# One-pass products for the output projection and eleven query blocks, and the routing spread over 36 expert blocks

## The chip, the cores and the metric

The kernel runs on one core of a Trainium2 chip. The metric is the time on the device in microseconds (us). Three runs of the kernel before gave a median of 989.1 us (988.98 to 989.2). A profiled execution stands beside them; all rows below come from it.

## What is computed

One decoder layer over 256 positions of width 1024, in float32. Attention in three groups of heads (block-compressed, selected and windowed; a top-64 selection by an indexer; 256 memory tokens), then an output projection, a normalisation, and PEER: 8 retrieval heads over 128 x 128 experts.

```python
x1 = layer_norm(alpha * x + concat(nsa, dsa, mem) @ w_out)     # 256 x 1024 by 1024 x 1024
qh = (x1 @ w_query).reshape(T, 8, 256)                         # 1024 x 2048: 16 blocks of 128 columns
s1, s2 = qh[..., :128] @ sub_keys_1.T, qh[..., 128:] @ sub_keys_2.T
# top 16 of each, top 16 of their sums: 16 experts and a softmax gate for each head
a = gelu(x1 @ expert_u.T)                                      # here: all 16384 experts, densely
y = (gate_matrix * a) @ expert_v
out = layer_norm(alpha * x1 + y)
```

The kernel doesn't gather experts. It computes all of them and multiplies by a gate matrix that is zero outside the chosen ones.

## The kernel before, in words

**Numbers.** A float32 matmul (`F32`) is run by TensorE as two records. A "one-pass" product takes operands rounded to `F32R`, and one record each. To keep precision an operand is split: ScalarE copies it into an `F32R` tile (its high part), VectorE or GpSimd subtracts that from the original (its low part), and TensorE adds high x high, high x low and low x high. Before the change the input projection, the expert blocks and the expert outputs are computed so; the output projection and the queries are plain `F32`.

**Engines and order.** Each engine has its own instruction list, written out by hand in the order of issue, and waits on semaphores. TensorE's list is the longest: attention units (`scores(u)`, `turn(u)`, `outputs(u)`, 20 of them) with slices of other work between them by `advance(work, n)`: `filler` (rest of the input projection, memory projections), `hidden` (compression), `mix0` and `mix1` (output projection of token blocks 0 and 1, 16 slices each). `turn_out(t, part)` transposes the attention output through PSUM bank 2, ScalarE copies it out (`save_out_turn`), and `mix(t)` multiplies it by `w_out`. VectorE normalises (`norm_sum`, `norm_centre`, `norm_scale`, with a root from ScalarE between), TensorE transposes x1 (`turn_x1`), ScalarE copies it (`save_x1_turn`).

**Queries.** `query(j)`, j = 0 to 31: 16 blocks of 128 columns for token block 0, then the same for token block 1 (the weights are loaded twice, through a ring of seven tiles). A query step is 8 matmuls of 128 columns; the step before's `subkey_scores` follows it. ScalarE saves both. VectorE finds the top 16 of each 128 scores, two query blocks at a time (`subkey_tops`), and `route(t)` combines them.

**Expert blocks.** `expert_in(c)`, c = 0 to 127: 24 one-pass products of 256 columns (8 slices of x1 by three). Its weights are loaded by SyncE into five tiles, high parts by ScalarE (`u_split`, three tiles), low parts by VectorE (`fill`), or by GpSimd for the blocks in `POOL_LOW` (5, 8, ... 23). VectorE still routes while the first blocks run; `FILL_AT` says after which of its steps (`pace`) the low part of which block comes. Before block `NTURN` = 30 TensorE transposes the routes (`turn_routes`, L922); ScalarE saves them (L1212), VectorE makes the tables (L1748, L1750).

**Gate groups.** The gate matrix is built in 64 groups of four tokens. For a group GpSimd writes six or five one-hot tiles of 128 x 128 (L467: two in `pair`; L471: four or three in `hot`), ScalarE scales and writes some (`pairs`), VectorE writes four (L1758), and TensorE does four one-pass products (`gates(g)`). Two buffers hold the one-hots, so GpSimd can be two groups ahead. ScalarE and VectorE take the result out (`save_low`, `gate_group`), and `block_gate(c)` multiplies the newly computed blocks. `GROUP_AT` says before which block each group stands: 64 groups from block 33 to block 123.

**Expert outputs.** `expert_out(c)`: 12 one-pass products of 512 columns a block, with splits of the weights by ScalarE (L1256) and VectorE.

L489 is the helper through which all matmuls but the transposes go; L1079 is `u_split`, L1570 `fill`.

Of the kernel before, what the change touches and what calls it, by code (L numbers as in the profile page):

```python
# [7 lines left out]
F32 = mybir.dt.float32  # L8
# [42 lines left out]
GROUP_AT = [N0 + g * (123 - N0) // 63 for g in range(GN)]  # L51
# [80 lines left out]
A_V = A_ALL - 1024  # L132

# [15 lines left out]
FIRST_HI = (22, 23, 26)  # L149


def peer_layer_kernel(nc, x, xT, memT, positions, w_tok, w_memq, w_memk, w_memv, w1k, w1v, w2k, w2v, peT,
                      w_out, ln1, wq, subk, uT, pv, ln2, consts, out):
    with ExitStack() as ctx:
# [68 lines left out]
        qT = gel[:, 0, :].rearrange("p (b t) -> p b t", b=2)  # L223
# [14 lines left out]
        w_o = ar(A_WOUT, KD * D).rearrange("p (k n) -> p k n", k=KD)  # L238
        ring = ar(A_RING, RING * 1024).rearrange("p (b n) -> p b n", b=RING)
# [5 lines left out]
        oT = [rawf[:, 1024 * t:1024 * (t + 1)] for t in range(T)]  # L245
# [53 lines left out]
        l_ring = [sem(f"l_ring{b}") for b in range(RING)]  # L299
# [21 lines left out]
        topped = sem("topped")  # L321
        g_shift, g_exp, route_ready = sem("g_shift"), sem("g_exp"), sem("route_ready")
# [48 lines left out]

        def v_slot(c):
            return (c + 4) % VR
# [8 lines left out]
        def _(sp):  # L382
# [29 lines left out]
            for j in range(RING - 2):  # L412
                load_query(j)
# [3 lines left out]
            for j in range(RING - 2, RING):  # L417
                load_query(j)
            sp.wait_ge(neg_ready, last_of(1, "dsa") + 1)
            sp.dma_start(xs[:, 1, :], x[:, 1, :]).then_inc(l_x, 16)  # L420
            for j in range(RING, 22):
                load_query(j)
# [4 lines left out]
            for j in range(22, 28):  # L427
                load_query(j)
# [3 lines left out]
            for j in range(28, 4 * PH):  # L432
                load_query(j)
# [21 lines left out]
        def _(pool):  # L455
# [7 lines left out]
            def onehots(g):  # L463
# [8 lines left out]
                ins.then_inc(pool_hot, 1)  # L472

# [13 lines left out]
        def _(pe):  # L487
# [188 lines left out]
            def turn(u):  # L676
# [38 lines left out]
            def turn_out(t, part):  # L715
# [4 lines left out]
                pe.wait_ge(pT_saved, nth("o", t, part))  # L720
                for i in range(4):
# [4 lines left out]
            def mix(t):  # L726
                parts = (0, 1)
                pe.wait_ge(l_wo, 16)
# [4 lines left out]
                for part in parts:  # L733
# [21 lines left out]
            def subkey_scores(j):  # L755
                pe.wait_ge(q_saved, j + 1)
                if j >= 1:
                    pe.wait_ge(sk_saved, j)
                mm(ps[:, 3, 0:P], qT[:, j % 2, :], subk_sb[:, j % 2, :], True, True).then_inc(pe_sk, 1)

            def query(j):
                t = j // (2 * PH)
                if j == 0:
                    pe.wait_ge(l_sk, 16)
                    pe.wait_ge(cmp_added, T)
# [1126 lines left out]
```

## Time and profile before

| | |
|---|---|
| median of runs | 989.1 us |
| the profiled execution's own time | 990.93 us |
| its span (first to last instruction) | 989.1 us |
| TensorE busy | 976.0 us, 99% |
| VectorE, ScalarE, GpSimd busy | 758.3, 531.6, 311.5 us |
| share of the chain that ended last in L489 on TensorE | 87% |
| granted clock of TensorE | 0.997 |

Busy time of TensorE is modelled from pipelined matmuls, and the duration listed for one matmul contains its pipeline; the distance between the starts of successive rows is its pace. In a timeline row "x16" is a run of 16 records, and brackets give idle time before the row and what ended it.

### The profile page before, as it was taken

Reading aid. Unit: us, or ns where it says so; the run is one execution under the profiler, and the core shown is the slowest. Engines: PE = TensorE matmul, PEld = TensorE weight load, DVE = VectorE, ACT = ScalarE, POOL = GpSimd, SP = SyncE. Lnnn points to the kernel's source line nnn. Section 1 sums busy time; section 2 is a strip of 40 time slices with the busy share of each in tenths; the row PEclk is TensorE's granted clock in tenths of the full one; section 3 lists DMA queues with packets and bytes.
Section 4 is the critical chain, followed back from the end, with each engine's and each line's share of the span. In section 5 each row is a group of like instructions: output and inputs, shape, how many; then the busy total and the mean of one; then the engine's idle time right before and its main releaser. Section 6 shows DMA issues by size and latency. Waiting matters only on the chain.

```text
span 989.1 us, 17661 instructions
## 1 busy us (share of the span) xinstructions
PE 976.0 (99%) x6306; PEld 871.3 (88%) x6306; DVE 758.3 (77%) x1875; ACT 531.6 (54%) x1125; POOL 311.5 (31%) x370
## 2 busy tenths in 40 slices
PE   9999999999999999999999999999999999999997
PEld 4888866999999999999999999988888888888885
DVE  4577635799998888889999999666666666666667
ACT  3555432234446888878888887633333333333341
POOL 1000000000220999999999999000000000000000
PEclk9999999999999999999999999999999999999999
DMA  9383201882555445444445444775555656555551
GB/s 327 143 349 129 88 20 56 256 328 99 180 191 173 158 163 171 167 154 165 161 167 165 161 167 154 252 234 192 193 192 195 196 193 196 195 193 192 192 191 43
DMA packets 48807, 176.52 MB, mean 178 GB/s; under 512 B 5185, under 2 KB 6225, under 8 KB 47569
## 3 DMA queue, kind: packets, MB, share of 16 engines
q1 hardware_dynamic: 48320, 173.82, 51.8%
q0 software_dynamic: 400, 1.58, 0.5%
q8 instruction: 51, 0.84, 0.3%
q14 instruction: 36, 0.29, 0.1%
HBM read 174.33 MB, written 1.05 MB: 177 GB/s over the span
## 4 chain that ended last, share of the span: by engine, by line
PE 89%; DVE 7%; DMA 2%; ACT 1%; issue 1%; SPq 1%
PE ps L489 87%; DMA arena<-in_w_tok 2%; DVE lo L1570 1%; PE ps L682 1%; DVE pair L1758 1%; DVE arena L1703 1%; DVE hi L1570 1%; DVE arena L1708 1%; DVE arena L1711 0%; ACT hi L1079 0%; SPq L387 0%; DVE slab L1768 0%; DVE arena L1772 0%; SPq L384 0%; SPq L385 0%
## 5 line engine op out<-in xcount | busy, mean ns | idle before, releaser
L489 PE MATMUL ps<-x1hl,hi 128*128 128x256 f32 x2248 | 374.1, 283 | 0.6 <-DVE hi L1570 0.6
L489 PEld LDWEIGHTS ps<-x1hl,hi 128*128 128x128 f32 x2248 | 330.2, 192 | 1.0 <-DVE hi L1570 0.8
L489 PE MATMUL ps<-hi,ahl 128*128 128x512 f32 x992 | 265.3, 389 | 0.0
L1256 ACT CAST hi<-slab 128x1024 fp32r<-128x1024 f32 x128 | 134.9, 1054 | 204.9 <-PE ps L489 204.9
L489 PE MATMUL ps<-x1hl,lo 128*128 128x256 f32 x824 | 233.1, 283 | 0.0
L489 PEld LDWEIGHTS ps<-hi,ahl 128*128 128x128 f32 x992 | 186.1, 188 | 38.6
L471 POOL TENSOR_SCALAR hot<-slab 128x128 fp32r<-128x128 f32 x224 | 197.5, 896 | 0.0
L489 PEld LDWEIGHTS ps<-x1hl,lo 128*128 128x128 f32 x824 | 158.1, 192 | 0.0
L1791 DVE TENSOR_TENSOR lo<-slab,hi 128x1024 fp32r<-128x1024 f32 x128 | 155.9, 1218 | 0.0
L489 PE MATMUL ps<-lo,ahl 128*128 128x512 f32 x496 | 152.8, 389 | 0.0
L1570 DVE TENSOR_TENSOR lo<-slab,hi 128x1024 fp32r<-128x1024 f32 x97 | 121.9, 1257 | 19.1 <-ACT hi L1079 18.8
L1079 ACT CAST hi<-slab 128x1024 fp32r<-128x1024 f32 x128 | 133.4, 1042 | 0.0
L1803 DVE CAST ahl<-arena 128x256 fp32r<-128x256 f32 x124 | 36.5, 294 | 102.3 <-PE ps L489 102.3
L489 PEld LDWEIGHTS ps<-lo,ahl 128*128 128x128 f32 x496 | 93.1, 188 | 19.3
L467 POOL TENSOR_SCALAR pair<-slab 128x128 fp32r<-128x128 f32 x128 | 95.3, 754 | 30.5 <-DVE slab L1750 26.3
L489 PE MATMUL ps<-arena 128*128 128x128 f32 (+6 forms) x806 | 102.3, 294 | 2.6 <-DVE arena L1301 1.4
L489 PEld LDWEIGHTS ps<-arena 128*128 128x128 f32 (+2 forms) x806 | 91.3, 192 | 10.3 <-issue 6.3
L476 POOL TENSOR_TENSOR lo<-slab,hi 128x1024 fp32r<-128x1024 f32 x6 | 14.4, 2405 | 267.5 <-ACT hi L1079 267.5
L1758 DVE TENSOR_SCALAR pair<-slab 128x128 fp32r<-128x128 f32 x256 | 77.6, 362 | 0.0
L1201 ACT ACTIVATE arena<-ps 128x256 f32<-128x256 f32 (+45 forms) x123 | 36.8, 299 | 46.5 <-PE ps L489 46.5
L1805 DVE TENSOR_TENSOR ahl<-arena,ahl 128x256 fp32r<-128x256 f32 x124 | 52.8, 425 | 4.4
L489 PE MATMUL ps<-arena,slab 128*128 128x512 f32 (+1 forms) x160 | 51.9, 470 | 0.7 <-ACT slab L1051 0.7
(209 smaller groups left out, 989.9 us busy)
## 6 DMA issues: line engine op xcount, KB each, us to landing
slab<-in_uT SPq DMA_DIRECT2D x128, 512.0 KB, 3.3
slab<-in_pv SPq DMA_DIRECT2D x128, 512.0 KB, 3.3
arena<-in_wq SPq DMA_DIRECT2D x32, 512.0 KB, 5.2
arena<-in_w_tok SPq DMA_DIRECT2D x8, 512.0 KB, 9.5
arena<-in_w_out SPq DMA_DIRECT2D x1, 4096.0 KB, 15.6
arena<-in_w_tok SPq DMA_DIRECT2D x1, 2048.0 KB, 15.5
arena<-in_w_tok SPq DMA_DIRECT2D x1, 1792.0 KB, 19.0
slab<-in_xT SPq DMA_DIRECT2D x4, 256.0 KB, 7.5
```

What stands on the lines that cost most here:

```text
L467: ins = nc.gpsimd.tensor_scalar(pair[:, g % 2, q, 1, :], iota, tbl[:, 4 * g + q, 0:1], None, ALU.is_equal)
L471: ins = nc.gpsimd.tensor_scalar(hot2[:, g % 2, q, :], iota, tbl[:, 4 * g + q, 1:2], None, ALU.is_equal)
L476: nc.gpsimd.tensor_tensor(u_rest_of(c), u_raw(c), hi[:, c % UH, :].bitcast(F32), ALU.subtract).then_inc(u_lo_pool, 1)
L489: return nc.tensor.matmul(o, lhsT, rhs, start=start, stop=stop, skip_group_check=True)
L1079: nc.scalar.copy(hi[:, c % UH, :], u_raw(c)).then_inc(u_hi, 1)
L1201: ins = nc.scalar.activation(arena[:, c * S + n:(c + 1) * S], ps[:, c % 2, n:S], ACT.Gelu)
L1256: nc.scalar.copy(hi[:, v_hi_slot(c), :], raw[:, v_slot(c), :]).then_inc(v_hi, 1)
L1570: v.tensor_tensor(u_rest_of(c), u_raw(c), hi[:, c % UH, :].bitcast(F32), ALU.subtract).then_inc(u_lo, 1)
L1758: ins = v.tensor_scalar(pair[:, g % 2, q, part, :], iota, tbl[:, 4 * g + q, 0:1], tbl[:, 4 * g + q, 2 + part:3 + part], ALU.is_equal, ALU. ...
L1791: v.tensor_tensor(lo[:, v_slot(c), :], raw[:, v_slot(c), :], hi[:, v_hi_slot(c), :].bitcast(F32), ALU.subtract).then_inc(v_lo, 1)
L1803: v.tensor_copy(o[:, 0, :], a).then_inc(a_hi, 1)
L1805: v.tensor_tensor(o[:, 1, :], a, o[:, 0, :].bitcast(F32), ALU.subtract).then_inc(a_lo, 1)
```

## The change

**Output projection.** `w_out` is split into high parts (ScalarE, `split_mix`, eight) and low parts (GpSimd, eight); the transposed attention output into high (`save_out_turn`, ScalarE) and low (`low_out`, VectorE, four). Each slice's one product becomes three one-pass products, the low x high ones gathered at every fourth slice. Bank 2 may be used again only after the low part is out.

**Queries.** Of 16 query blocks the first five (`ALONE`) are still computed for each token block alone, in plain `F32`; the other eleven for both token blocks at once, by 24 one-pass products of 256 columns. The order is in `STEPS`: 5 alone for token block 0, 11 joint, 5 alone for token block 1; 21 steps instead of 32 and 21 weight loads. High parts of the weights are ScalarE's (`split_query`), low parts VectorE's for the first five joint steps (`low_query`), GpSimd's for the other six. The x1 split moves ahead: `split_x1` for token block 0, `high_x1` and `low_x1` straight from PSUM for token block 1, and `keep_x1` saves it for the last steps. The second `turn_x1` comes before step 4 instead of step 14. Weights 3 to 5 are loaded after the last attention unit, 6 to 9 after half of `mix1` (`pe_half`), later ones when a tile is free. The searches alternate between the token blocks.

**Routing and groups.** The numbers at the top of the diff. `POOL_LOW` stays as it was. ScalarE's `base_of_sums` moves from blocks 124 and 125 to block 126.

The orders of all lists between the attention units are rearranged; the diff leaves those out but for the end of TensorE's.

```diff
-N0 = 33
-NROUTE = 29
-NTURN = 30
-FILL_AT = (54, 55, 57, 66, 68, 68, 76, 79, 79, 86, 89, 89, 97, 99, 99, 106, 109, 109, 119, 120, 120, 123, 124,
-           124, 127, 128, 129, 130, 131,)
+N0 = 40
+NROUTE = 36
+NTURN = 37
+FILL_AT = (59, 61, 72, 73, 74, 74, 77, 78, 78, 80, 81, 81, 83, 84, 84, 86, 89, 89, 96, 99, 99, 106, 109, 109,
+           119, 120, 122, 123, 124, 125, 126, 127, 128, 129, 130, 131,)
 GN = S // 4
 UR, UH = 5, 3
 VR, VH = 8, 4
-GROUP_AT = [N0 + g * (123 - N0) // 63 for g in range(GN)]
+GROUP_AT = [N0 + g * (125 - N0) // 63 for g in range(GN)]
...
+ALONE = 5
+A_WQH, WQH = A_EQ, 5
+A_MORE, MORE = A_WQH + WQH * D, 3
+OWN = ALONE + 5
+assert A_MORE + MORE * D <= A_WMQ
+STEPS = ([(0, j) for j in range(ALONE)] + [(T, j) for j in range(ALONE, 2 * PH)]
+         + [(1, j) for j in range(ALONE)])
+SCORED = [(t, j) for who, j in STEPS for t in range(T) if who in (t, T)]
...
-FIRST_HI = (22, 23, 26)
+FIRST_HI = (18, 19, 21)
...
-            def load_query(j):
-                if j >= RING:
-                    sp.wait_ge(pe_q, j - RING + 1)
-                sp.dma_start(ring[:, j % RING, :], wq[j % (2 * PH)]).then_inc(l_ring[j % RING], 16)
+            def load_query(n):
+                if n >= RING + MORE:
+                    sp.wait_ge(pe_q, n - RING - MORE + 1)
+                elif n >= 6:
+                    sp.wait_ge(pe_half, 1)
+                elif n >= 3:
+                    sp.wait_ge(pe_pv, NU)
+                sp.dma_start(query_raw(n), wq[STEPS[n][1]]).then_inc(query_here(n)[0], 16)
...
+            for k in range(KD):
+                pool.wait_ge(wo_hi, k + 1)
+                nc.gpsimd.tensor_tensor(w_o_lo[:, k, :], w_o[:, k, :], w_o_hi[k // 4][:, k % 4, :].bitcast(F32),
+                                        ALU.subtract).then_inc(wo_lo, 1)
+
+            for n in range(OWN, 2 * PH):
+                pool.wait_ge(q_hi, n - ALONE + 1)
+                nc.gpsimd.tensor_tensor(query_low(n), query_raw(n),
+                                        wq_hi[:, n % WQH, :].bitcast(F32), ALU.subtract).then_inc(q_lo_pool, 1)
...
+                if parts_turned(nth("u", u)):
+                    pe.wait_ge(o_lo, parts_turned(nth("u", u)))
...
                     pe.wait_ge(pT_saved, nth("o", t, part) + 1)
+                    if t == 0:
+                        pe.wait_ge(wo_lo, 4 * part + 4)
                     for half in range(2):
+                        cs = slice(half * 512, (half + 1) * 512)
                         for k in range(4 * part, 4 * part + 4):
-                            first, final = (part, k % 4) == (parts[0], 0), (part, k % 4) == (parts[1], 3)
-                            last = mm(ps[:, 4 * (1 - t) + half, :], oT[t][:, k * P:(k + 1) * P],
-                                      w_o[:, k, half * 512:(half + 1) * 512], first, final)
-                            if final:
+                            a_high, a_low = (o[:, t, k * P:(k + 1) * P] for o in (oT_hi, oT_lo))
+                            w_high, w_low = w_o_hi[part][:, k % 4, cs], w_o_lo[:, k, cs]
+                            if half == 0 and k % 4 == 3:
+                                pe.wait_ge(o_lo, parts_turned(nth("o", t, part)) + 1)
+                            for m, (a, w) in enumerate(((a_high, w_high), (a_high, w_low))):
+                                mm(ps[:, 4 * (1 - t) + half, :], a, w, part == 0 and k == 0 and m == 0, False)
+                            for kl in {0: (), 1: (), 2: (), 3: range(k - 3, k + 1)}[k % 4]:
+                                last = mm(ps[:, 4 * (1 - t) + half, :], oT_lo[:, t, kl * P:(kl + 1) * P],
+                                          w_o_hi[part][:, kl % 4, cs], False, part == 1 and kl == 7)
+                            if k == 7:
                                 last.then_inc(pe_mix, 1)
+                            if t == 1 and half == 1 and k == 3:
+                                last.then_inc(pe_half, 1)
                             yield
...
+            def query(n):
...
+                if n == ALONE:
+                    pe.wait_ge(x1_split, 2 * T)
+                if n == 2 * PH:
+                    pe.wait_ge(x1_kept, 2)
+                pe.wait_ge(*query_here(n))
+                if who == T and n < OWN:
+                    pe.wait_ge(q_lo, n - ALONE + 1)
+                elif who == T:
+                    pe.wait_ge(q_lo_pool, n - OWN + 1)
...
+                    if who < T:
+                        last = mm(ps[:, 4 + n % 2, 0:P], w[:, ks], x1T[who][:, k, :], k == 0, k == KD - 1)
+                    else:
+                        for m, (a, part) in enumerate(((w_high, 0), (w_high, 1), (w_low, 0))):
+                            last = mm(ps[:, 4 + n % 2, 0:S], a[:, ks], x1hl[:, k, part, :], k == 0 and m == 0,
+                                      k == KD - 1 and m == 2)
...
             outputs(19)
             advance(mix0, 1)
             turn_out(1, 0)
-            advance(mix0, 1)
+            advance(mix0, 2)
             advance(mix1, 8)
             turn_out(1, 1)
             advance(mix1, 4)
             turn_x1(0)
             advance(mix1, 4)
-            for j in range(4 * PH):
-                if j == 2 * PH - 2:
+            for n in range(len(STEPS)):
+                if n == ALONE - 1:
                     turn_x1(1)
-                query(j)
-            subkey_scores(4 * PH - 1)
+                query(n)
+            subkey_scores(len(STEPS) - 1)
...
+            def split_mix(k):
+                act.wait_ge(l_wo, 16)
+                if k >= 4:
+                    act.wait_ge(pe_memp, 6)
+                nc.scalar.copy(w_o_hi[k // 4][:, k % 4, :], w_o[:, k, :]).then_inc(wo_hi, 1)
...
+            def split_query(n):
+                act.wait_ge(*query_here(n))
+                if n == ALONE:
+                    act.wait_ge(pe_pv, NU)
+                if n >= ALONE + WQH:
+                    act.wait_ge(pe_q, n - WQH + 1)
+                nc.scalar.copy(wq_hi[:, n % WQH, :], query_raw(n)).then_inc(q_hi, 1)
...
             save_out_turn(1, 1)
+            split_query(5)
             root(0)
+            split_query(6)
+            split_query(7)
+            split_query(8)
             save_x1_turn(0)
-            for j in range(4 * PH):
-                if j == 2:
+            split_query(9)
+            for n in range(len(STEPS)):
+                if n in FIRST_HI:
+                    u_split(FIRST_HI.index(n))
+                save_query(n)
+                if n == 0:
                     root(1)
-                if j == 2 * PH - 2:
-                    save_x1_turn(1)
-                if j in FIRST_HI:
-                    u_split(FIRST_HI.index(j))
-                save_query(j)
-            save_scores(4 * PH - 1)
+                if n == ALONE - 2:
+                    high_x1()
+                    keep_x1()
+                if ALONE + WQH <= n + WQH < 2 * PH:
+                    split_query(n + WQH)
+            save_scores(len(STEPS) - 1)
+            if len(STEPS) in FIRST_HI:
+                u_split(2)
...
+                if c == 126:
+                    base_of_sums(0)
+                    base_of_sums(1)
                 if c >= NK - VH:
...
+            low_out(1, 0)
             weights(1, "mem")
             scale_pair(1)
             dve.wait_ge(l_x, 16)
             dve.wait_ge(l_ln1, 16)
             norm_sum(0)
             norm_centre(0)
+            low_out(1, 1)
+            low_query(5)
             norm_scale(0)
+            low_query(6)
+            low_query(7)
+            low_query(8)
+            low_query(9)
             dve.wait_ge(l_x, 32)
             norm_sum(1)
             norm_centre(1)
             norm_scale(1)
```

## Rows read from the trace of the kernel before

**Rows 1.** Windows from first tables to last one-hot; columns: busy us and count per engine.

```profile
core 0: us, PE busy (x) PEld busy (x) DVE busy (x) ACT busy (x) POOL busy (x), PEclk, DMA share, GB/s
320.70:616.20 295.50, 294.28 (x2444) 293.33 (x2443) 272.86 (x620) 247.17 (x650) 290.56 (x352) 1.00 0.49 163
```

**Rows 2.** Timeline of TensorE, output projection, queries, first expert block; columns: start, duration.

```profile
147.81 8.04 PE L489 MATMUL ps<-arena,slab 128*128 128x512 f32 x18
...
155.69 0.60 PE L722 MATMUL ps<-slab 128*128 128x128 f32 x4
...
164.81 3.73 PE L489 MATMUL ps<-arena 128*128 128x128 f32 x32
...
168.60 1.95 PE L489 MATMUL ps<-arena 128*128 128x128 f32 x16
...
170.39 0.39 PE L489 MATMUL ps<-slab,gel 128*128 128x128 f32 x2
...
170.61 1.95 PE L489 MATMUL ps<-arena 128*128 128x128 f32 x16
...
230.60 0.48 PE L489 MATMUL ps<-x1hl,hi 128*128 128x256 f32 x2
```

**Rows 3.** Timeline of TensorE, late gate groups, and a window of the expert outputs.

```profile
609.75 0.64 PE L489 MATMUL ps<-pair,hot 128*128 128x256 f32 x4
...
613.11 0.64 PE L489 MATMUL ps<-pair,hot 128*128 128x256 f32 x4
...
619.35 0.64 PE L489 MATMUL ps<-pair,hot 128*128 128x256 f32 x4
...
634.23 0.63 PE L489 MATMUL ps<-hi,ahl 128*128 128x512 f32 x2
...
640.00:900.00 260.00, 260.00 (x1149) 215.29 (x1148) 177.69 (x288) 101.18 (x96) 0.60 (x1) 1.00 0.60 197
```

**Rows 4.** ScalarE's copy by timeline, groups of the page, and a DMA issue line.

```profile
156.32 0.58 ACT L1051 COPY slab<-ps 128x512 f32<-128x512 f32 x1 [7.72 <-PE ps L722]
...
L1079 ACT CAST hi<-slab 128x1024 fp32r<-128x1024 f32 x128 | 133.4, 1042 | 0.0
...
L476 POOL TENSOR_TENSOR lo<-slab,hi 128x1024 fp32r<-128x1024 f32 x6 | 14.4, 2405 | 267.5 <-ACT hi L1079 267.5
...
arena<-in_wq SPq DMA_DIRECT2D x32, 512.0 KB, 5.2
```

**Rows 5.** GpSimd's one-hots beside VectorE's low part; waits of L467; window of L1570.

```profile
593.05 0.60 POOL L467 TENSOR_SCALAR pair<-slab 128x128 fp32r<-128x128 f32 x1
...
594.21 0.97 POOL L471 TENSOR_SCALAR hot<-slab 128x128 fp32r<-128x128 f32 x1
...
595.15 1.33 POOL L471 TENSOR_SCALAR hot<-slab 128x128 fp32r<-128x128 f32 x1
...
602.00 1.17 POOL L467 TENSOR_SCALAR pair<-slab 128x128 fp32r<-128x128 f32 x2
...
611.56 1.18 POOL L467 TENSOR_SCALAR pair<-slab 128x128 fp32r<-128x128 f32 x2
...
612.72 3.47 POOL L471 TENSOR_SCALAR hot<-slab 128x128 fp32r<-128x128 f32 x4
...
594.71 1.31 DVE L1570 TENSOR_TENSOR lo<-slab,hi 128x1024 fp32r<-128x1024 f32 x1
...
  PE ps L489: 4.1, 7
...
321.40:616.20 294.80, 115.47 (x91) 1.00 0.49 163
```

**Rows 6.** Timelines about the turn of the routes: TensorE, VectorE, GpSimd.

```profile
318.10 0.82 PE L922 MATMUL ps<-slab,arena 128*128 128x128 f32 x6
...
327.39 0.64 PE L489 MATMUL ps<-pair,hot 128*128 128x256 f32 x4
...
320.23 0.41 DVE L1748 CAST slab<-slab 128x256 fp32r<-128x256 f32 x1 [2.89 <-ACT slab L1212]
...
321.43 1.26 POOL L467 TENSOR_SCALAR pair<-slab 128x128 fp32r<-128x128 f32 x2 [26.27 <-DVE slab L1750]
```

More of the change, by code:

```diff
@@ L370, in pool_lows, with parts_turned, query_raw, query_low @@
             return sum(b <= c for b in POOL_LOW)
+        def parts_turned(n):
+            return sum(event[0] == "o" for event in TURNS[:n])
+        def query_raw(n):
+            b = (n + 4) % (RING + MORE)
+            return ring[:, b, :] if b < RING else more[:, b - RING, :]
+        def query_low(n):
+            b = (n + 4) % (RING + MORE)
+            return ring_lo[:, b, :] if b < RING else more_lo[:, b - RING, :]
+        def query_here(n):
+            return l_ring[n % (RING + MORE)], (n // (RING + MORE) + 1) * 16
         def v_slot(c):
@@ L753, in turn_x1, with subkey_scores @@
                     last.then_inc(pe_pT, 1)
[L755 to L763, printed above, removed]
+            def subkey_scores(n):
+                who, j = STEPS[n]
+                pe.wait_ge(q_saved, n + 1)
+                if n >= 1:
+                    pe.wait_ge(sk_saved, sum(2 if w == T else 1 for w, _ in STEPS[:n]))
+                for i in range(2 if who == T else 1):
+                    last = mm(ps[:, 3, i * P:(i + 1) * P], qT[:, n % 2, i * P:(i + 1) * P], subk_sb[:, j % 2, :], True, True)
+                last.then_inc(pe_sk, 1)
@@ L789, in _ @@
             turn_tokens()
[L790 removed]
+            advance(filler, 3)
             index_scores()
[L792 removed]
+            advance(filler, 6)
             scores(0)
[L794 removed]
+            advance(filler, 5)
             scores(2)
             turn(0)
[L797 to L809 removed]
+            advance(filler, 3)
+            outputs(0)
+            turn(1)
+            advance(filler, 3)
+            turn(2)
+            scores(4)
+            outputs(1)
+            advance(filler, 2)
+            outputs(2)
+            advance(filler, 2)
+            turn(3)
+            advance(filler, 4)
             outputs(3)
             advance(filler, 1)
+            turn(4)
             turn_later(0)
@@ L814, in _ @@
             turn_later(1)
-            turn(4)
             advance(filler, 3)
@@ L821, in _ @@
             outputs(4)
+            index_later(0)
             scores(8)
+            outputs(5)
             turn(6)
-            index_later(0)
             turn(7)
-            outputs(5)
             outputs(6)
+            scores(10)
             index_later(1)
+            turn(8)
+            advance(hidden, 4)
             outputs(7)
-            turn(8)
-            scores(10)
-            advance(hidden, 4)
             outputs(8)
@@ L835, in _ @@
             advance(filler, 1)
+            advance(hidden, 8)
+            advance(filler, 2)
+            advance(hidden, 4)
+            advance(filler, 4)
             turn(9)
+            advance(hidden, 8)
+            turn(10)
             advance(hidden, 4)
+            outputs(9)
+            advance(filler, 9)
+            turn(11)
             advance(filler, 1)
-            advance(hidden, 8)
-            advance(filler, 9)
-            advance(hidden, 8)
-            outputs(9)
-            advance(hidden, 4)
-            advance(filler, 5)
-            turn(10)
             scores(12)
-            turn(11)
+            advance(filler, 1)
             outputs(10)
-            advance(filler, 5)
             outputs(11)
+            advance(filler, 2)
+            compress_kv()
             scores(14)
+            advance(filler, 2)
             turn(12)
-            compress_kv()
-            advance(filler, 6)
-            cmp_scores(0)
-            advance(filler, 4)
-            outputs(12)
-            advance(filler, 1)
-            turn(13)
+            advance(filler, 3)
+            cmp_scores(0)
+            advance(filler, 1)
+            outputs(12)
+            turn(13)
+            advance(filler, 6)
+            turn(14)
+            cmp_turn(0)
             scores(16)
-            cmp_turn(0)
-            turn(14)
             outputs(13)
             turn(15)
+            outputs(14)
             cmp_out(0)
-            outputs(14)
             outputs(15)
@@ L1655, in _ @@
             scale_pair(0)
+            low_out(0, 0)
+            low_out(0, 1)
             maxima(18)
@@ L1671, in _ @@
             norm_scale(1)
-            split_x1(0)
-            for b in range(0, 10, 2):
+            split_x1()
+            low_x1()
+            for b in range(0, ALONE, 2):
                 subkey_tops(0, b)
```

218 lines of the change are left out of this document (121 added, 97 removed).

## The prediction

> **What bounds the kernel now.** I read the page first: TensorE is busy for 99% of the span, and nearly the whole chain of waits is its matmuls. An average says nothing about a stage, so next came the windows, from the opening of the gate tables to GpSimd's last one-hot [rows 1]: there TensorE is at 294.3 of 295.5 us and GpSimd at 290.6, VectorE at 272.9. Two engines are full at once, and one that is made faster alone will meet the other. The reader is to see this double bound; the change touches only TensorE's side of it.
>
> Then the timelines, for the real pace of instructions (the listed duration of a matmul contains its pipeline). A query step of before takes 2.01 us, 168.60 to 170.61: 16 records of fp32 in 1.79 and the subkey product in 0.22 [rows 2]. The output projection runs 18 records from 147.81 to 155.69, 0.438 us each [rows 2]. One-pass products are in the trace too: an expert block and a gate group go from 609.75 to 613.11, 28 records of 256 columns in 3.36 us, 0.12 each, so 2.88 a block and 0.48 a group; and with 512 columns 1149 records fill 260 us, 0.226 each [rows 3].
>
> **TensorE's own work.** Output projection: 32 products of two records, 64 x 0.438 = 28.0 us, become 96 x 0.226 = 21.7: 6.3 less. Queries: 32 steps x 2.01 = 64.3 us become 10 single steps (20.1) and 11 joint ones of 24 x 0.12 + 2 x 0.22 = 3.33 (36.6): 7.6 less. Together 13.9 us less, and the expert blocks could start that much earlier than 230.60 [rows 2].
>
> **What of that is lost before the experts.** Three places.
> First, filler. The first half of the projection fills the gaps of attention's last units, in which TensorE waits for copies. Its 14.0 us become 10.9, while a part now needs ScalarE's copy (0.59 [rows 4]) and VectorE's subtraction before bank 2 is free. Bounds: nothing lost, or all 3.1 and 2 waits of 0.7 on top. I take 1.5.
> Second, the first norm. Call H the second turn of token block 1's output; in before it stands at 155.69 and the queries begin at 164.81, H + 9.1 [rows 2]. Now ScalarE has, between that copy and its copy of x1: four high parts of 1.04 us [rows 4] and the root, and three of the four wait for weights whose DMAs are issued only at about H, 5.2 us to landing [rows 4]. By my count: copy until H + 1.2, high part of 5 until 2.3, root 3.9, of 6 to 8 until about 8.1 (landings 1.5 apart), x1 copied at 9.2. TensorE has its own work until 9.2, so the second half's gain of 1.5 us is gone and no more.  If the loads land 3 us later, all of it is on the path.
> Third, the second norm now has only four query steps in front of its turn instead of fourteen. VectorE must do four low parts at 1.27 (115.5 us over 91 [rows 5]) first: x1 ready at about H + 17.6, where TensorE is at H + 17.4; the joint steps start at H + 21.0 where they could at 20.5. I take 1.7 for it, since the copies in between come as late; low bound 0, high bound 5.
> Sum: 13.9 - 1.5 - 1.5 - 1.7 = 9.2. Experts start at 221.4, bounds 216.7 (nothing lost) and 226.
> ScalarE's eight high parts of the output weights (8.3 us) and GpSimd's eight low parts (2.4 each by [rows 4], 19.2) lie beside attention, where GpSimd is empty; I cost them at nothing, and at up to 2 us if exponentials queue behind them. GpSimd's six query low parts, 2.4 in a step of 3.33, are hidden. In VectorE's queue the candidate searches come in pairs per two joint steps and follow TensorE; u blocks 2 and 3 are loaded when the searches of block 0 of the tokens are through, some 3 us before use.
>
> **Routing.** Its time is set by no engine's work but by a place in TensorE's order: the turn of the routes. In before it stands ahead of block 30, at 318.10; VectorE had finished and waited 2.89 us for the saved table; GpSimd's first one-hot follows at 321.43 [rows 6]. That is 90.8 after the expert start. The change puts the turn ahead of block 37: 7 x 2.88 = 20.2 later, 111.0 after the start. VectorE gets seven low parts more (8.8 us) and has 20.2 us more for them. So GpSimd begins at 221.4 + 111.0 = 332.4, 11 us later than now. This is the term that the reader should watch: TensorE has become earlier, GpSimd later.
>
> **The gate groups.** TensorE alone: first group at 96.8 after the start [rows 6], now 117.0; then 85 blocks instead of 90 and 63 groups, 85 x 2.88 + 63 x 0.48 = 275.0; then one group and three blocks (9.1): 401.1 after the start. (Before: 634.23 - 230.60 = 403.6 [rows 2, 3].)
> GpSimd: 64 groups took 321.43 to 616.2, of which 4.1 us were waits for TensorE [rows 5, 6]: 290.7, or 4.54 a group. A one-hot in the clear has a pitch of 0.58 (two from 593.05 to 594.21); beside VectorE's low part at 594.71 the two one-hots take 0.97 and 1.33, and 1.1 us are lost [rows 5]. 352 one-hots x 0.58 = 204; the other 86.5 us over 91 low parts [rows 5] is 0.95 each. With some 87 low parts in the stage: 204 + 83 = 287, or 4.48 a group, against 275.0/63 = 4.37 that TensorE would take. GpSimd is the bound: last one-hot at 332.4 + 287 = 619.4, group 63 at 619.7, + 9.1 = 628.8. Bounds of a low part's toll: 0 (TensorE then binds, 622.5) and the full 1.27 (then 314 us, 656).
> A page of the Trainium skill speaks against this change: GPSIMD Engine Reference, Key points, says that GpSimd shares its SBUF interfaces with VectorE and contends with VectorE's instructions in a 2-port mode or with two SBUF inputs. By that rule the toll at 594.71 was to be expected, and VectorE's gating products and one-hots could tax GpSimd too; what they would do here is in rival C.
> VectorE: 272.9 us less seven low parts and the small products of those blocks, 262 in 287: 91%, but fuller towards the end. ScalarE has 15% to spare.
>
> **The end.** After group 63 come three blocks instead of five, in which ScalarE scales x (four copies, 2.4 us), the first v block lands (3.3 us after its issue) and is split. I count 8.2 us against 8.6 available: nothing, up to 2 us; I add 0.5. The expert outputs are unchanged.
> Sum: 628.8 - 634.2 + 0.5 = -4.9. The profiled execution took 990.93 (span 989.1), so 986.0; the runs' median is 1.8 below it: **984.2 us**.
>
> **Rivals.**
> A. TensorE binds all through, because one-hots dodge the low parts. For: GpSimd waited 7 times for TensorE in before [rows 5]. Against: only 4.1 us, and it now starts 11 us later. 221.4 + 401.1 = 622.5: 978; with nothing lost before the experts, 973.
> B. The stages before the experts give nearly nothing: late weights in front of the x1 copy, then the second norm. Start at 226 to 228, end at 634: 989. For: four weight loads at H; against: my count has TensorE busy beside most of it.
> C. Slower: the gate stage goes at its old pace. One mechanism: VectorE's low parts, gating products and one-hots, packed denser, hold up GpSimd's one-hots more often, and a group needs both engines. The point is 4.60 us a group (332.4 + 294.4 + 9.4 = 636.2, 991). At 4.66: 995. For: the two groups from 602.00 to 611.56 took 4.78 each [rows 5]. Against: the average of all 64 was 4.54, and fewer low parts fall in each now.
> D. GpSimd's low parts do not change: the diff leaves their list as it stood, so from that part of the title comes nothing; in the sum it is 0.
>
> **Chances.** Forecast (980 to 987) 0.53, A 0.15, B 0.14, C 0.18. What a measurement of this kernel tells from no change is about 0.2%, 2 us. Faster than 987.1: most of the forecast, all of A, a little of B: 0.68. Within: 0.15. Slower: C nearly whole, 0.17. Range 978 to 992: A's and C's near ends are in.
>
> **What would show it.** Records of a joint step 0.12 apart, of the projection 0.226. First expert matmul at 219 to 224. First one-hot 111 after it, later than 321.43 on the clock. GpSimd over 98% busy without waits for TensorE, and TensorE with 5 to 8 us of gaps at gate groups, released by GpSimd or VectorE. End of the expert blocks 407 after their start; 401 speaks for A, 413 and more for C. I am wrong if the start does not move, or if GpSimd is seen waiting.

## The result, and the profile after

The changed kernel took 992.72 us in the median of 17 runs (990.16 to 999.2), the kernel before 989.27 us beside it (17 runs, 988.98 to 990.8): a ratio of 1.0045, 95% interval 1.0034 to 1.0057. The forecast was 984.2, faster; it is slower by 3.5 us, outside the range. The profiled execution took 993.19 us, its span is 991.4, 2.3 above the span of before.

The page first: GpSimd is now on the chain that ended last, as the prediction had it, and TensorE is busy 967.4 us, 8.6 less than before. It does less and ends later.

```profile
span 991.4 us, 17517 instructions
...
PE 967.4 (98%) x6250; PEld 871.3 (88%) x6250; DVE 778.6 (79%) x1877; ACT 548.8 (55%) x1130; POOL 341.7 (34%) x384
...
PE 66%; POOL 27%; DVE 3%; DMA 2%; SPq 1%; ACT 1%; issue 1%; DVEq 0%
```

TensorE's timeline gives the milestones, in order: two waits within attention, the second turn of token block 1's output (H of the prediction; 155.69 before [rows 2]), the queries (164.81 [rows 2]), a joint step with its products, the first expert block (230.60 [rows 2]), the turn of the routes (318.10 [rows 6]), the last gate group (619.35 [rows 3]) and the expert outputs (634.23 [rows 3]).

```profile
114.90 1.08 PE L532 MATMUL ps<-slab,arena 128*128 128x32 f32 x8 [1.89 <-DVE arena L1561]
...
132.80 1.12 PE L769 MATMUL ps<-slab 128*128 128x128 f32 x4 [4.59 <-DVE slab L1649]
...
161.53 0.60 PE L769 MATMUL ps<-slab 128*128 128x128 f32 x4
...
170.79 3.81 PE L532 MATMUL ps<-arena 128*128 128x128 f32 x32
...
181.71 0.50 PE L532 MATMUL ps<-x1hl,wq_hi 128*128 128x256 f32 x2
...
182.16 0.40 PE L532 MATMUL ps<-x1hl,wq_hi 128*128 128x256 f32 x2
...
182.52 0.40 PE L532 MATMUL ps<-x1hl,wq_hi 128*128 128x256 f32 x2
...
229.20 0.48 PE L532 MATMUL ps<-x1hl,hi 128*128 128x256 f32 x2
...
335.83 0.82 PE L995 MATMUL ps<-slab,arena 128*128 128x128 f32 x6
...
627.40 0.64 PE L532 MATMUL ps<-pair,hot 128*128 128x256 f32 x4
...
636.52 0.63 PE L532 MATMUL ps<-hi,ahl 128*128 128x512 f32 x2
```

The reader is to take differences. From H to the first expert block are 67.7 us, and 68.9 by the sum. H itself stands at 152.5 by the sum: 155.69, less 4.7 for the 24 of the projection's 32 slices that lie ahead of it (three quarters of 6.3), plus the 1.5 of loss. It came at 161.53, 9.0 us late. So the search is before H. There the timelines of GpSimd and of VectorE (start, duration) stand side by side:

```profile
110.34 2.35 POOL L509 TENSOR_TENSOR w_o_lo<-arena,w_o_hi 128x1024 fp32r<-128x1024 f32 x1 [8.69 <-ACT w_o_hi L1130]
123.48 6.98 POOL L509 TENSOR_TENSOR w_o_lo<-arena,w_o_hi 128x1024 fp32r<-128x1024 f32 x3 [10.79 <-ACT w_o_hi L1130]
```

```profile
110.97 1.75 DVE L1609 TENSOR_SCALAR slab<-slab 128x2 f32<-128x2 f32 x1
...
118.62 0.17 DVE L1609 TENSOR_SCALAR slab<-slab 128x2 f32<-128x2 f32 x1
...
123.80 0.43 DVE L1605 CUSTOM_DVE_ANT_0 arena<-ps,xs 128x256 f32<-128x256 f32 x1 [3.87 <-PE ps L532]
...
124.61 1.26 DVE L1609 TENSOR_SCALAR slab<-slab 128x2 f32<-128x2 f32 x1
...
126.58 1.60 DVE L1609 TENSOR_SCALAR slab<-slab 128x2 f32<-128x2 f32 x1
...
128.32 2.16 DVE L1617 TENSOR_TENSOR slab<-slab 128x8 f32<-128x8 f32 x1
130.52 1.63 DVE L1633 SCALAR_TENSOR_TENSOR slab<-ps,slab 128x64 f32<-128x64 f32 x8
132.06 0.68 DVE L1649 TENSOR_TENSOR slab<-ps,slab 128x512 f32<-128x512 f32 x1
```

An operation on two numbers a partition takes 0.17 us at 118.62, and 1.75, 1.26 and 1.60 beside GpSimd's low parts of `w_out`. Each long one ends where a low part ends: GpSimd's low part of 110.34 at 112.69, VectorE's operation at 112.72; of the three from 123.48 (2.33 each) the ends are at 125.8, 128.1 and 130.46, VectorE's at 125.87, 128.18 and 130.48. The extra times of the last three, 1.09 + 1.43 + 2.0 = 4.5 us, are TensorE's wait of 4.59 at 132.80: it waits for L1649, behind them in VectorE's list. The operation at 123.80, which also reads PSUM, wasn't held.

Nor is every operation within SBUF held. VectorE beside another low part, GpSimd's row first:

```profile
99.29 2.36 POOL L509 TENSOR_TENSOR w_o_lo<-arena,w_o_hi 128x1024 fp32r<-128x1024 f32 x1 [6.56 <-ACT w_o_hi L1130]
99.44 0.43 DVE L1530 MAX8 slab<-xs 128x8 f32<-128x256 f32 x1
100.43 0.20 DVE L1614 RECIPROCAL slab<-slab 128x8 f32<-128x8 f32 x1
100.66 1.01 DVE L1617 TENSOR_TENSOR slab<-slab 128x8 f32<-128x8 f32 x1
```

`MAX8` and `RECIPROCAL` take here what they take elsewhere (0.43, 0.19 to 0.20); the `TENSOR_TENSOR` behind them, 0.17 elsewhere, lasts until GpSimd's end at 101.65.

Then the clock. Windows of 5 us (busy us per engine, then PEclk, TensorE's granted clock as a share of full speed): it was at full speed in all of these in the kernel before. A share of 0.74 or 0.71 in a window that TensorE fills costs 1.3 or 1.5 us.

```profile
110.00:115.00 5.00, 3.11 (x17) 2.31 (x15) 4.44 (x12) 2.03 (x7) 2.35 (x1) 1.00 0.00 0
115.00:120.00 5.00, 5.00 (x28) 4.50 (x29) 3.58 (x14) 1.91 (x6) 0.00 (x0) 0.74 0.00 0
120.00:125.00 5.00, 4.82 (x31) 3.82 (x29) 1.17 (x5) 2.92 (x5) 1.52 (x1) 0.92 0.01 2
125.00:130.00 5.00, 3.20 (x24) 2.96 (x24) 4.93 (x8) 3.61 (x11) 5.00 (x3) 1.00 0.15 39
130.00:135.00 5.00, 2.20 (x10) 1.70 (x12) 4.03 (x13) 0.58 (x1) 0.45 (x1) 0.61 0.18 68
135.00:140.00 5.00, 5.00 (x22) 3.55 (x19) 1.19 (x3) 0.59 (x1) 0.00 (x0) 0.71 0.00 0
```

With and behind the two waits a part of TensorE's time ran at the lower level, 1.2 GHz. Low parts, held operations, waits, clock: four steps. That the waits bring the clock down isn't shown by itself: the kernel before has such a stretch too, in which TensorE was busy throughout and which the changed kernel lacks (1.00 from 100 to 105):

```profile
100.00:105.00 5.00, 5.00 (x22) 4.10 (x24) 0.10 (x1) 2.15 (x5) 0.00 (x0) 0.68 0.72 256
```

### The profile page after: what moved, and what is told of

The parts are those of the page before. It is cut to its first block, busy times and chain, and to the rows that moved or that the text cites. A ratio compares the mean times of both kernels' runs of the same rounds, so it can differ in the third digit from the quotient of the medians.

```text
span 991.4 us, 17517 instructions
## 1 busy us (share of the span) xinstructions
PE 967.4 (98%) x6250; PEld 871.3 (88%) x6250; DVE 778.6 (79%) x1877; ACT 548.8 (55%) x1130; POOL 341.7 (34%) x384
## 4 chain that ended last, share of the span: by engine, by line
PE 66%; POOL 27%; DVE 3%; DMA 2%; SPq 1%; ACT 1%; issue 1%; DVEq 0%
PE ps L532 64%; POOL hot L504 18%; POOL pair L500 9%; DMA arena<-in_w_tok 2%; PE ps L727 1%; SPq L419 0%; DVE slab L1609 0%; DVE arena L1605 0%; SPq L416 0%; DVE xs L1523 0%; PE ps L769 0%; DVE slab L1617 0%; SPq L417 0%; PE ps L807 0%; PE ps L609 0%
## 5 line engine op out<-in xcount | busy, mean ns | idle before, releaser
L504 POOL TENSOR_SCALAR hot<-slab 128x128 fp32r<-128x128 f32 x224 | 193.6, 878 | 0.0
L1707 DVE TENSOR_TENSOR lo<-slab,hi 128x1024 fp32r<-128x1024 f32 x97 | 122.7, 1266 | 17.7 <-ACT hi L1181 17.6
L1321 ACT ACTIVATE arena<-ps 128x256 f32<-128x256 f32 (+43 forms) x125 | 38.1, 305 | 55.5 <-PE ps L532 55.4
L532 PE MATMUL ps<-arena 128*128 128x128 f32 (+7 forms) x454 | 59.4, 311 | 1.7 <-DVE arena L1422 1.4
L509 POOL TENSOR_TENSOR w_o_lo<-arena,w_o_hi 128x1024 fp32r<-128x1024 f32 x8 | 18.9, 2376 | 121.2 <-ACT w_o_hi L1130 121.2
L532 PEld LDWEIGHTS ps<-arena 128*128 128x128 f32 (+2 forms) x454 | 50.2, 194 | 9.2 <-issue 5.5
L532 PE MATMUL ps<-pair,hot 128*128 128x256 f32 x256 | 42.5, 289 | 3.6 <-POOL hot L504 1.6
```

The source lines that it names most:

```text
L504: ins = nc.gpsimd.tensor_scalar(hot2[:, g % 2, q, :], iota, tbl[:, 4 * g + q, 1:2], None, ALU.is_equal)
L509: nc.gpsimd.tensor_tensor(w_o_lo[:, k, :], w_o[:, k, :], w_o_hi[k // 4][:, k % 4, :].bitcast(F32), ALU.subtract).then_inc(wo_lo, 1)
L532: return nc.tensor.matmul(o, lhsT, rhs, start=start, stop=stop, skip_group_check=True)
L1321: ins = nc.scalar.activation(arena[:, c * S + n:(c + 1) * S], ps[:, c % 2, n:S], ACT.Gelu)
L1707: v.tensor_tensor(u_rest_of(c), u_raw(c), hi[:, c % UH, :].bitcast(F32), ALU.subtract).then_inc(u_lo, 1)
```

## Experiments

Ten kernels ran. Theory 1: GpSimd's low parts of `w_out` are what makes H late, by holding VectorE. Rivals: the new order of attention, the other parts of the change, or the low parts merely coming late.

**Queries only.** Everything of the change but the output projection, with the lists of attention in their old order.

```diff
-  a_high x w_high, a_high x w_low, a_low x w_high      # mix(t)
+  oT[t] x w_o, plain F32; no split_mix, no low_out; lists of PE, ACT, DVE as before up to turn_out(1, 0)
```

> Only the query part, the routing over 36 blocks and the group numbers of the change; the output projection in plain F32 and the order of all lists up to it are those of before. Theory 1 (GpSimd's low parts of w_out hold up VectorE in the attention stage) and rival 2 (the new order and the thinner one-pass filler cost the time there) both expect the second turn of token block 1's output at 155.7 as in before, experts 67.7 us behind it at 223.4 (229.2 in the changed kernel), and 407 us from there to the end of the expert blocks: some 986 to 987, 6 less than the changed kernel. If the experts start after 227, the loss lies in the query part and both are wrong.

986.33 us (985.68 to 987.72; ratio 0.997, 0.996 to 0.9981). H at 155.93, experts at 223.86, outputs at 631.03, 407.2 after. So the query, routing and group parts are worth 3 us, and in the changed kernel the projection's part turns them into a loss.

**No low parts of w_out.** The changed kernel; GpSimd's eight low parts are left out, and TensorE multiplies by the high part twice, so this part of the product is missing.

```diff
-  nc.gpsimd.tensor_tensor(w_o_lo[:, k, :], w_o[:, k, :], w_o_hi..., ALU.subtract).then_inc(wo_lo, 1)   # eight times
-  pe.wait_ge(wo_lo, 4 * part + 4)
+  pe.wait_ge(wo_hi, 4 * part + 4)
-  w_high, w_low = w_o_hi[part][:, k % 4, cs], w_o_lo[:, k, cs]
+  w_high, w_low = w_o_hi[part][:, k % 4, cs], w_o_hi[part][:, k % 4, cs]
```

> The changed kernel without GpSimd's eight low parts of w_out; TensorE does as many products as before (high x high twice), so the low parts of w_out are left out of the result. Theory 1: VectorE's small instructions fall back from 1.3 to 2.2 us to 0.2, the wait of 4.6 us before the first output turn goes, and with it the stretches at half clock; the second output turn at 153 to 156 instead of 161.5, time 984 to 987. Rival 2 (order and filler): second turn after 159, time 990 to 993. Rival 3 (ScalarE's high parts queue ahead of its exponentials): as rival 2, since they stay.

983.52 us (982.13 to 987.53; 0.9944, 0.9929 to 0.996). The timeline has H at 150.77, and no wait at the first turn of that output (124.40; 132.80 in the changed kernel):

```profile
112.65 1.08 PE L527 MATMUL ps<-slab,arena 128*128 128x32 f32 x8 [0.31 <-DVE arena L1556]
...
124.40 0.66 PE L764 MATMUL ps<-slab 128*128 128x128 f32 x4
...
150.77 0.60 PE L764 MATMUL ps<-slab 128*128 128x128 f32 x4
```

and VectorE's small operations are short again:

```profile
121.61 0.17 DVE L1604 TENSOR_SCALAR slab<-slab 128x2 f32<-128x2 f32 x1
121.69 0.20 DVE L1609 RECIPROCAL slab<-slab 128x8 f32<-128x8 f32 x1
121.92 0.17 DVE L1612 TENSOR_TENSOR slab<-slab 128x8 f32<-128x8 f32 x1
```

H is 10.8 us earlier, more than theory 1 had asked for. TensorE's full work is there, and so are ScalarE's high parts and the new order: none of these makes H late. The 10.8 by the two traces: 0.7 was there before the first low part (a place in TensorE's list at 56.70 against 56.02, another at 111.11 against 110.44), so that 10.1 are the low parts'. Of these 6.2 are waits (1.89 + 4.59 - 0.31); the other 3.9 fit the clock, some 4.1 by the windows (1.3 + 1.5; 0.4 in 120 to 125, at 0.92; 0.9 in 130 to 135, 0.39 of 2.2 us busy). In this kernel every window of 5 us from 90 to 170 is at full clock.

**Pieces.** The low parts are back on GpSimd, all of them, each cut into eight instructions of 128 columns. It keeps the amount of work and changes only the length of one instruction.

```diff
-  nc.gpsimd.tensor_tensor(w_o_lo[:, k, :], ...).then_inc(wo_lo, 1)
+  for c in range(0, D, 128):
+      ins = nc.gpsimd.tensor_tensor(w_o_lo[:, k, c:c + 128], ...)
+  ins.then_inc(wo_lo, 1)
```

> The changed kernel with each of GpSimd's eight low parts of w_out cut into eight instructions of 128 columns (2.4 us becomes eight of about 0.35). Theory 1, in the form that an instruction of GpSimd with two SBUF inputs shuts VectorE's SBUF-to-SBUF instructions out until it ends: VectorE's small instructions now wait 0.3 us at most, the second output turn comes at 152 to 156 instead of 161.5, experts at 220 to 224, time 984 to 987. Rival 4, that the total of GpSimd's traffic slows VectorE: nothing gained, or worse by the fixed cost of 56 more instructions, 992 to 996.

985.54 us (983.52 to 988.01; 0.9961, 0.9949 to 0.9974). GpSimd's timeline, and then VectorE's:

```profile
121.24 10.03 POOL L511 TENSOR_TENSOR w_o_lo<-arena,w_o_hi 128x128 fp32r<-128x128 f32 x24 [6.62 <-ACT w_o_hi L1133]
```

```profile
123.30 0.51 DVE L1612 TENSOR_SCALAR slab<-slab 128x2 f32<-128x2 f32 x1
123.72 0.19 DVE L1617 RECIPROCAL slab<-slab 128x8 f32<-128x8 f32 x1
123.94 0.27 DVE L1620 TENSOR_TENSOR slab<-slab 128x8 f32<-128x8 f32 x1
```

GpSimd is busy longer (0.42 a piece, 3.4 a low part against 2.35), and yet H comes at 153.43, 8.1 earlier. The longest of the 20 small operations of that line is 0.53 us (1.75 in the changed kernel). That settles how VectorE is held: until the running GpSimd instruction ends.

**Low parts on VectorE.** The whole change, with the low parts in idle places of VectorE's list, and attention in its old order.

```diff
-  GpSimd: eight low parts
+  DVE: low_mix(0..3) between rounds of index_round(1), low_mix(4..7) beside cmp_shift(1)
```

> The whole change, but the eight low parts of w_out are VectorE's, in its idle places, and the lists up to the projection are ordered as in before. Theory 1: nothing shuts VectorE out; second output turn at 152 to 155 (155.9 in the run with the queries alone, less the first half's one-pass gain, plus what ten us more on VectorE push back), experts at 220 to 223, and the gate stage as before 407.3: 984 to 986. Rival 2 (one-pass filler is too thin for the copies behind bank 2): not below 986.

985.25 us (984.53 to 986.29; 0.9963, 0.9949 to 0.9977). H at 152.19, outputs at 627.67. The same result by moving the work (1.22 us a low part on VectorE); its one wait for a low part is 0.85 us.

**Old order, low parts on GpSimd.** The same kernel with the eight low parts given back to GpSimd: against the last one it moves nothing else.

```diff
-  DVE: low_mix(0..7)
+  GpSimd: the loop of the changed kernel
```

> The whole change, w_out's low parts on GpSimd as in it, but the lists of attention in the order of before (those of the kernel with VectorE's low parts, with the low parts taken from VectorE's list). Theory 1 (GpSimd's low parts hold VectorE's small operations, wherever the lists put these): small VectorE operations of over 1 us beside GpSimd's low parts, second turn of token block 1's output at 155 to 161, 987 to 992 us. Rival (it is the new order of attention that makes the low parts costly, by putting the softmax's small operations on the path beside them): the turn at 152 to 153 as with VectorE's low parts, 985. The spread of the runs is read too: 1 to 2 us, if the new order makes it; up to 9 us, if GpSimd's low parts do.

989.69 us (987.68 to 991.53; 1.0003, 0.9994 to 1.0011), H at 157.34, 5.1 later than with VectorE's. The size is as theory 1 has it, but the reason is mostly another one. Waits of TensorE and GpSimd's timeline:

```profile
139.75 0.77 PE L532 MATMUL ps<-w_o_hi,oT_hi 128*128 128x512 f32 x1 [3.94 <-POOL w_o_lo L509]
```

```profile
130.20 9.41 POOL L509 TENSOR_TENSOR w_o_lo<-arena,w_o_hi 128x1024 fp32r<-128x1024 f32 x4 [31.19 <-ACT w_o_hi L1129]
```

Four low parts in a row take GpSimd 9.4 us where VectorE takes 4.7, and TensorE waits 3.94 for the last, 3.1 more than for VectorE's. Behind it the clock is at 0.72 from 140 to 145, 1.4 us more. Single small operations are held here too (1.87, 1.23 and 2.40 us), but off the path: no wait of TensorE ends with them. So theory 1 has a condition: the hold costs where the list puts small operations beside low parts and on the path, as the new order does; the old order pays the slowness of GpSimd instead.

**New order alone.** Plain projection as in the first experiment, with the lists in the new order.

```diff
-  lists of PE, ACT, DVE as before up to turn_out(1, 0)
+  lists of the changed kernel, without split_mix and low_out
```

> The query part of the change with the plain projection, in the new order of the lists. Against the run with the queries alone in the old order it shows what the order costs: theory 1 expects nothing or little (second output turn 154 to 157, 985 to 988), rival 2 a second turn after 159 (990 or more).

988.82 us, but 986.78 to 998.84 in ten runs (1.0009, 0.9986 to 1.0033). The profiled execution took 986.78: H at 154.85, a microsecond earlier than in the old order (which has its clock at 0.66 from 100 to 105, the new order at 1.00). In the trace the order costs nothing; in the runs it scatters over 12 us where the old order stays within about 2, and its median is 2.5 us above. The scatter goes with TensorE's mean granted clock: the four runs of up to 987.51 have 0.998 or 0.999, that of 991.57 has 0.993, that of 998.84 has 0.986. From end to end that is 12 us, and 0.012 of a span of 985 is 11.8.

**One more one-hot of every second group on ScalarE.** The changed kernel with 320 one-hots for GpSimd instead of 352.

```diff
-ACT_HOT = ((0,), ())
+ACT_HOT = ((0,), (0,))
```

> The changed kernel with one one-hot more of every second group written by ScalarE, so that GpSimd writes five per group throughout (320 instead of 352). If GpSimd binds the gate stage, it needs 32 x 0.58 = 18.6 us less than its 287, TensorE takes over at 401 us from the start of the experts to their end instead of 407.3: 6 less, about 986.5. If VectorE or ScalarE bind it (ScalarE gets 22 us more and is then over 90% busy): no change or slower, 992 to 995.

988.14 us, nine of ten runs in 985.61 to 993.9 and one at 1001.06 with a clock of 0.980 (0.9996, 0.9976 to 1.0015): not to be told from before, but faster than the change, whose interval (1.0034 to 1.0057) lies apart. The profiled execution took 987.72, 5.5 less than that of the change. H stays late (160.78), and outputs come 402.7 after the experts instead of 407.3. The window of its one-hots:

```profile
338.20:616.80 278.60, 277.74 (x2302) 276.45 (x2301) 264.10 (x606) 248.00 (x695) 260.57 (x320) 1.00 0.49 162
```

GpSimd drops to 260.6 of 278.6 us and TensorE fills 277.7: GpSimd had been the bound, and TensorE follows 4.6 us behind. I had expected 6 us, with TensorE at 401 from the experts to the outputs; it takes 402.7.

**The same edit with the plain projection.**

```diff
-ACT_HOT = ((0,), ())
+ACT_HOT = ((0,), (0,))        # in the kernel of the first experiment
```

> The query, routing and group parts of the change with the plain output projection, and both one-hots of the second column of each group's first pair on ScalarE (320 one-hots left for GpSimd instead of 352). Theory 1 (the low parts of w_out in attention and GpSimd's one-hot chain are two separate costs that add): start of the experts at 223.9 as in the kernel with plain projection, outputs 402.7 after it as in the changed kernel with the same edit: outputs at 626.6, 981 to 982.5 us. Rival (the edit's 4.6 us in the gate stage were won only because that stage had started late): outputs 407 after the start, 986.

982.11 us (981.16 to 982.94; 0.9924, 0.991 to 0.9938); experts at 223.54, outputs 402.7 later. The two costs are separate and add, as theory 1 says.

**The turn of the routes at block 34.** The changed kernel with the turn, and the first group, three blocks earlier.

```diff
-N0 = 40
-NROUTE = 36
-NTURN = 37
+N0 = 37
+NROUTE = 33
+NTURN = 34
# FILL_AT without its last three steps
```

> The changed kernel with the routes turned ahead of block 34 instead of 37, routing over 33 blocks and the groups from block 37 on (to 125 as in the change). If the place of the turn sets GpSimd's start, its first one-hot comes 8.6 us earlier (330.5) and its last at about 618; TensorE then binds at 401: 6 less, 986.5. Rival: VectorE isn't through with routing at block 34, the turn waits, TensorE idles, and nothing is gained: 991 to 994.

1001.31 us (994.08 to 1003.79; 1.0106, 1.007 to 1.0143), and the first one-hot still comes 109.3 after the experts' start. My theory fell, the rival was right and too mild:

```profile
326.25 0.29 DVE L1888 TENSOR_TENSOR arena<-arena 128x128 f32<-128x128 f32 x1
326.46 1.22 DVE L1706 TENSOR_TENSOR lo<-slab,hi 128x1024 fp32r<-128x1024 f32 x1
...
327.73 0.79 PE L531 MATMUL ps<-x1hl,hi 128*128 128x256 f32 x2 [5.19 <-DVE lo L1706]
...
333.02 1.09 PE L994 MATMUL ps<-slab,arena 128*128 128x128 f32 x6
```

TensorE starves 5.19 us for a low part that VectorE reaches only behind its last step of routing (L1888, ended 326.5), and the turn follows no earlier. The turn's place in TensorE's order decides only as long as VectorE is through with its routing and with the low parts of the blocks ahead, and three blocks earlier it isn't; another `FILL_AT` for this turn wasn't tried. The profiled execution took 996.34; the three runs above 1001 have a clock of 0.984 to 0.986 against its 0.992, which is about their difference (0.006 of 1000 us).

**The version that beats both.** VectorE's low parts and the 320 one-hots together.

```diff
-  GpSimd: eight low parts;  ACT_HOT = ((0,), ())
+  DVE: low_mix(0..7), attention in its old order;  ACT_HOT = ((0,), (0,))
```

> The run before with ScalarE writing one one-hot of every group. Both findings together: experts at 220 to 223 and 402.7 us from there to the end of the expert blocks as in the run with that edit alone: 979 to 982. If the gate stage is then bound by VectorE or ScalarE: 984 to 986.

979.13 us (978.89 to 979.98; ratio 0.99, 0.9883 to 0.9916), 10 us faster than before and 13.6 than the change. H at 152.41, outputs at 622.64. Against the same edit with the plain projection (982.11) the one-pass projection is worth 3.0 us here.

## Why the prediction was wrong

The step that failed, in its words: "ScalarE's eight high parts of the output weights (8.3 us) and GpSimd's eight low parts (2.4 each by [rows 4], 19.2) lie beside attention, where GpSimd is empty; I cost them at nothing, and at up to 2 us if exponentials queue behind them." The high parts cost nothing that shows (H is at 150.77 with them and without the low ones). The low parts cost some 10 us at H: it is 161.53 against 150.77 without them, of which 0.7 is older than the first low part (160.02 and 160.78 in the two other profiled kernels with this attention). Against the H of the sum it is 9.0, since I had taken 1.5 us of filler as lost: with nothing lost the sum has H at 151.0, and without the low parts it came at 150.77. (The kernel before, from which I counted, lost 1.6 us to the clock at 100 to 105, so this agreement is in part luck.) "Where GpSimd is empty" was the wrong test: the cover was looked for on GpSimd, and the price was paid by VectorE. It could be asked of the trace before, since [rows 5] show the two engines taking time from each other; I used that for GpSimd's toll alone and never turned it round. The Trainium skill's GPSIMD Engine Reference, Key points, has it without direction: the two engines share SBUF interfaces and contend. The trace agrees, with VectorE as the loser (0.17 against up to 1.75 us for the same operation).

None of the rivals was this one. B comes nearest in size (start at 226 to 228), with another mechanism; on the slower side I had only C, the gate stage. C's numbers came out by chance (636.2 and 991; measured 636.52 and 992.72), its mechanism didn't: the stage ran at 4.49 us a group (287.4 over 64), not at 4.60.

The other steps, by row:

- **Paces.** A joint step's records are 0.12 apart (182.16 to 182.52, three records), the projection's 0.23 (163.15, 163.38, 163.61). Right.
- **H to the queries.** 9.26 us (161.53 to 170.79) against 9.2 to 9.4. Right: late weights were no cost.
- **Second norm.** Joint steps at H + 20.2, forecast H + 21.0. Right within a microsecond; of the 1.7 us that the sum takes for it, 1.2 weren't lost (H to experts 67.7, 68.9 by the sum).
- **Experts to first one-hot.** 229.20 to 339.17 is 110.0; forecast 111.0. VectorE's time to spare there is smaller than I took it for: with the turn at block 34 it is late.
- **Gate stage.** The window of GpSimd's one-hots, 287 us forecast; in the window its busy time is the whole of it, and it waited for nobody:

```profile
339.20:626.60 287.40, 283.83 (x2337) 281.07 (x2336) 269.38 (x613) 242.06 (x641) 287.40 (x352) 1.00 0.47 158
```

  87 low parts of VectorE lie in it, as counted, so the toll is (287.4 - 204)/87 = 0.96 us each, 0.95 before. TensorE idles 3.6 us in it, less than the 5 to 8 that I had named. Rivals A and C are out.
- **The end.** Last one-hot to outputs: 9.9 us (626.6 to 636.52), as in the sum (9.4 and 0.5). The 0.5 lies elsewhere than I had it: ahead of the last group (0.8 instead of 0.3), and not in the three blocks behind it (9.12, forecast 9.1). Experts to outputs: 407.3; the sum has 407.9.
- **D.** GpSimd's low parts of expert blocks: nothing, as said.

So 9.0 us of error at H are 7.8 at the experts' start (229.20 against 221.4) and 7.2 at the outputs (636.52 against 629.3 by the sum): GpSimd's start comes 1.0 sooner behind the experts', its stage is 0.4 longer. The median misses by 8.5: I took it to lie 1.8 below the profiled execution, as before, and it lies 0.5 below, which is the other 1.3. Against before: GpSimd's start 17.7 later (339.17, 321.43 [rows 6]), its stage 7.4 shorter (287.4, 294.8), what follows 8.1 shorter (9.9, 18.0): 2.3 later in all.

**Open.** Kernels with the new order of attention scatter (over 9, 15, 12 and 10 us in four, 5 in two) and those with the old one hardly (1 to 2 us; 4 with GpSimd's low parts). The plain projection in the new order has no low parts of `w_out` and scatters over 12 us, so they are not the cause alone. What the longer runs of a kernel have is a lower clock of TensorE: in the changed kernel the eleven runs of up to 993.19 us have 0.993 to 0.997, the six from 995.86 to 999.2 have 0.986 to 0.989. So the changed kernel gives away more clock than the kernel before (0.997 to 0.999): at the 0.993 of its median at most 6.9 us, an estimate (0.007 of its span, idle time counted in). What brings the clock down in the one order and hardly in the other, and where, isn't shown, since one execution of each was profiled. The median of the changed kernel lies 0.5 us below its profiled run, so the profile's account of the median doesn't hang on it.

## What to carry to other kernels

Work put on an idle engine isn't free until it is known what its instructions hold on other engines: look in the trace for instructions that are longer than their own kind beside it. A long GpSimd operation over SBUF belongs where VectorE has no small operations on the path, or is cut short; eight pieces cost GpSimd 1.0 us more each time and gave 7 us back. And when two engines are full, moving work from the one that binds (32 one-hots) gives only the distance to the next, here 4.6 us.

## What the runs showed of the hardware

- A GpSimd subtraction of 128x1024 (2.33 to 2.38 us) holds VectorE's `TENSOR_SCALAR` and `TENSOR_TENSOR` from SBUF to SBUF until it ends: 128x2 in 1.26 to 1.75 us, 128x8 in up to 2.16, in place of 0.17. Seven `SCALAR_TENSOR_TENSOR` of 128x256 took 8.0 us beside two of them, 4.0 without. Pieces of 128x128 (0.42 us) hold it at most to 0.53.
- Not each is held: the operation with an operand in PSUM at 123.80 took 0.43 beside it, 0.42 to 0.43 without it; within SBUF, `MAX8` (0.43), `RECIPROCAL` (0.20) and `TENSOR_REDUCE` (0.28) took the same with and without.
- The Trainium skill's GPSIMD Engine Reference, Key points, names two SBUF inputs, or a two-port mode, as the condition. The held operation on 128x2 has one tile as input, so two inputs aren't needed here; the runs don't show whether it is the mode.
- The other way about, one VectorE low part (1.28 us) costs GpSimd's one-hots 0.96 on average, in both kernels.
- Waits of 1.9 and 4.6 us in attention were followed by stretches at the lower level of TensorE's clock, some 4 us lost; about two fifths of what the low parts cost wasn't waiting at all. A wait isn't needed for it (before, 0.68 from 100 to 105 with TensorE busy throughout), nor is idle time always followed by it: with VectorE's low parts TensorE idled 1.25 us in 125 to 130, and the clock stayed at 1.00 there and behind.
- Between runs of one kernel the time goes with TensorE's mean granted clock: plain projection in the new order, 986.78 us at 0.998 and 998.84 at 0.986, about 1 us for each 0.001.
